# Stacking the high and low gate rows of the mLSTM into one matmul, and starting the output projection's buffers at multiples of 1 KB

## The reference

```python
def step(carry, xs):                      # one chunk of tokens, four heads
    b = jnp.cumsum(lfb, axis=-1)
    log_d = b[..., :, None] - b[..., None, :] + ib[..., None, :]
    log_d = jnp.where(causal, log_d, NEG)
    inter = b + m[..., None]
    m_t = jnp.maximum(jnp.max(log_d, axis=-1), inter)
    d_mat = jnp.exp(log_d - m_t[..., None])
    inter_w = jnp.exp(inter - m_t)
    s = jnp.einsum('bhtd,bhsd->bhts', qb, kb) * d_mat
    num = (jnp.einsum('bhts,bhsd->bhtd', s, vb)
           + inter_w[..., None] * jnp.einsum('bhvk,bhtk->bhtv', C, qb))
    ...
    C_new = decay[..., None, None] * C + jnp.einsum('bhs,bhsv,bhsk->bhvk', w, vb, kb)

mixed = jnp.concatenate([att.astype(x.dtype), ml, cv.astype(x.dtype)], axis=-1)
x = x + jnp.einsum('bse,ed->bsd', mixed, w_out[l])
```

## The kernel before

| tile | before | changed |
|---|---|---|
| `o_wh`, `o_wl`, `o_m`, `o_z`, `o_x` | 960 | 0 |
| `o_mh`, `o_ml`, `o_y` | 768 | 0 |
| moving operands of the spreads (`m_row_hi`, `m_row_lo`; then `m_row_parts`) | 0 | 256 |
| `m_mask_r` (moving, mask matmul) | 832 | 832 |
| `AHL`, `WH`, `WL` of the dense products | 0 | 0 |

## Time and profile before

### The profile page before, as it was taken

One profiled execution on the slowest core, in us unless ns is written; L12 is line 12 of the kernel. 1 busy time (PEld: TensorE's weight loads), 2 busy tenths in 40 slices (PEclk: granted clock), 3 DMA queues, 4 the chain that ended last, 5 costly groups with the idle time before them and its releaser, 6 DMA issues. The chain is left out here.

```text
span 3526.5 us, 43854 instructions
## 1 busy us (share of the span) xinstructions
PE 3339.7 (95%) x16481; PEld 2697.1 (76%) x16481; DVE 1839.3 (52%) x2219; ACT 1124.6 (32%) x1699; POOL 1436.1 (41%) x1006
## 2 busy tenths in 40 slices
PE   5877999999999999999999999999999999698899
PEld 5656878888888778888877888888778888376687
DVE  8785135544455776860125455455766860564421
ACT  4222133333333441112124333333541111566300
POOL 6810225656666322232225565666412231243421
PEclk9889999999999999999999999999999999898899
DMA  3344111111111222223211111111212231416543
GB/s 123 103 108 128 64 48 48 54 48 54 48 54 51 92 76 101 98 97 137 102 51 49 49 54 48 54 48 53 96 60 108 101 103 54 172 57 219 156 136 115
DMA packets 155316, 301.01 MB, mean 85 GB/s; under 512 B 16400, under 2 KB 91408, under 8 KB 153520
## 3 DMA queue, kind: packets, MB, share of 16 engines
q1 hardware_dynamic: 139056, 257.10, 22.9%
q10 hardware_dynamic: 16128, 42.08, 3.0%
HBM read 226.20 MB, written 72.94 MB: 85 GB/s over the span
## 5 line engine op out<-in xcount | busy, mean ns | idle before, releaser
L1721 PE MATMUL ps_job<-AHL,WH 128*128 128x512 f32 x4480 | 1382.1, 390 | 28.4 <-POOL WL L1290 26.8
L1290 POOL TENSOR_TENSOR WL<-WR,WH 128x1024 fp32r<-128x1024 f32 x216 | 523.0, 2422 | 1199.9 <-ACT WH L992 1198.4
L1721 PEld LDWEIGHTS ps_job<-AHL,WH 128*128 128x128 f32 x4480 | 840.8, 188 | 206.8 <-issue 19.0
L1721 PE MATMUL ps_job<-AHL,WL 128*128 128x512 f32 x2240 | 871.9, 389 | 0.0
L992 ACT CAST WH<-WR 128x1024 fp32r<-128x1024 f32 x216 | 226.9, 1051 | 1004.4 <-PE ps_job L1721 820.6
L1721 PEld LDWEIGHTS ps_job<-AHL,WL 128*128 128x128 f32 x2240 | 420.9, 188 | 87.4
L1481 DVE SCALAR_TENSOR_TENSOR ps_job<-ps_job,RB 128x1024 f32<-128x1024 f32 (+1 forms) x80 | 79.9, 1017 | 409.6 <-PE ps_job L1721 396.1
L1310 POOL TENSOR_TENSOR OPS_L<-VS,OPS_H 128x1024 fp32r<-128x1024 f32 (+2 forms) x96 | 193.9, 2036 | 55.8 <-ACT OPS_H L1118 51.3
L1400 DVE TENSOR_TENSOR VS<-ps_job,VS 128x1024 f32<-128x1024 f32 x16 | 19.6, 1225 | 362.3 <-PE ps_job L1721 362.3
L1818 PE MATMUL ps_job<-OPS_H,WH 128*128 128x512 f32 x512 | 199.5, 390 | 0.7 <-POOL WL L1290 0.7
L1818 PE MATMUL ps_job<-OPS_H,WL 128*128 128x512 f32 x512 | 199.3, 389 | 0.0
(11 more groups left out here) (428 smaller groups left out, 5732.8 us busy)
## 6 DMA issues: line engine op xcount, KB each, us to landing
WR<-in_wall SPq DMA_DIRECT2D x244, 512.0 KB, 3.5
fm_scratch<-VS ACTq DMA_DIRECT2D x32, 512.0 KB
tm_scratch<-VS ACTq DMA_DIRECT2D x28, 512.0 KB
s_U<-in_x_group SPq DMA_DIRECT2D x8, 1024.0 KB, 14.8
s_mt<-z_scratch SPq DMA_DIRECT2D x64, 128.0 KB, 4.5
prod_scratch<-s_Win SPq DMA_DIRECT2D x16, 512.0 KB, 2.6
X<-in_x_feat SPq DMA_DIRECT2D x2, 4096.0 KB, 14.8
m_oz<-tm_scratch SPq DMA_DIRECT2D x8, 1024.0 KB, 8.2
```

What stands on the lines that cost most here:

```text
L1290: pool.tensor_tensor(dst, raw, src.bitcast(F32), ALU.subtract).then_inc(raw_free, 1)
L1721: last = pe.matmul(out, l, r, start=(k == 0 and i == 0), stop=(k == k_tiles - 1 and i == 2))
```

## The change

Three things are done.

1. `load_pairs` brings each of the two row sets back from the DRAM scratch, twice: once into partitions 0 to 63 and once into partitions 64 to 127 of `m_row_pair0` and `m_row_pair1`. SP issues these four transfers in `attention`, behind the loads of the stage, and waits first until both stores of the rows have landed.
2. DVE makes the spread's operands 128 rows high: the high part in partitions 0 to 63 of `m_row_parts`, the low part in 64 to 127. For this it first adds two shifted pieces of the identity, and rounds both halves (the lower half into `m_row_hi`) before it subtracts. `spread` is then one matmul of 128 rows where it was two of 64.
3. `finish` places its buffers at multiples of 1 KB, and an unused buffer `o_w_pad` at the high end of SBUF does the same for those that come from there.

```diff
@@ attention
     env["weights"] = ExitStack()
+    env["weights"].enter_context(nc.sbuf_tensor("o_w_pad", [P, nc.sbuf_top % 1024 // 4], F32, side="right"))
     env["wh"] = wh = nc.alloc_sbuf_tensor_at("o_wh", [P, KD, D], F32R, offset=nc.sbuf_top)
...
             sp.dma_start(par[:], d["cv_par"]).then_inc(ld_p, 16)
+            rows.load_pairs(sp)
...
-            sp.wait_ge(rows.st, 32)
+            sp.wait_ge(rows.ld_pair, 64)
@@ GateRows
+        self.pair = [sb(f"m_row_pair{i}", [P, MC]) for i in range(2)]
...
+    def load_pairs(self, sp):
+        by_chunk = lambda v: v.rearrange("h (c n) -> (h c) n", n=MC)
+        sp.wait_ge(self.st, 32)
+        for i in range(2):
+            for part in range(2):
+                sp.dma_start(self.pair[i][part * self.n:(part + 1) * self.n], by_chunk(self.d["rows"][i])).then_inc(self.ld_pair, 16)
@@ mlstm_chunks
-            by_row = ident[0:R, 0:R].rearrange("p (h c) -> p h c", h=H)
...
+            dve.tensor_tensor(by_row[:], ident[:, high], ident[:, low], ALU.add).then_inc(of_set, 1)
...
-            for i, r in enumerate((rows.T, rows.B)):
+            for i, r in enumerate(rows.pair):
...
-                dve.tensor_copy(row_hi[i][:], by_head[i][:]).then_inc(row_set, 1)
-                dve.wait_ge(row_set, 3 * i + 2)
-                dve.tensor_tensor(row_lo[i][:], by_head[i][:], row_hi[i][:].bitcast(F32), ALU.subtract).then_inc(row_set, 1)
+                dve.tensor_copy(row_parts[i][high], by_head[i][high]).then_inc(row_set, 1)
+                dve.tensor_copy(row_hi[low], by_head[i][low]).then_inc(row_set, 1)
+                dve.wait_ge(row_set, 4 * i + 3)
+                dve.tensor_tensor(row_parts[i][low], by_head[i][low], row_hi[low].bitcast(F32), ALU.subtract).then_inc(row_set, 1)
...
             def spread(c, i, stop):
-                at = of_chunk[:, c:c + 1].to_broadcast([R, P])
-                pe.matmul(flat(e_ps[:]), at, flat(row_hi[i][:]), start=True, stop=False)
-                return pe.matmul(flat(e_ps[:]), at, flat(row_lo[i][:]), start=False, stop=stop)
+                return pe.matmul(flat(e_ps[:]), of_chunk[:, c:c + 1].to_broadcast([P, P]), flat(row_parts[i][:]), start=True, stop=stop)
@@ finish
-    sb, ps, sem = tools(nc, ctx)
+    sb, ps, sem = tools(nc, ctx, 1024)
```

More of the change, by code:

```diff
@@ L2417, in __init__ @@
         self.tok, self.dec = sb("m_tok", [P, N_MC, 3 * M_HEADS]), sb("m_dec", [P, M_HEADS, N_MC])
+        self.ld_pair = sem("m_ld_pair")
         self.ld, self.a_done, self.v_done, self.st, self.turned, self.tok_done = (
@@ L2537, in mlstm_chunks @@
     ident_r = sb("m_ident_r", [P, P], F32R)
-    of_head, in_chunk, of_chunk = sb("m_of_head", [R, H]), sb("m_in_chunk", [R, N_MC]), sb("m_of_chunk", [R, N_MC], F32R)
-    by_head = [sb(f"m_by_head{i}", [R, H, MC]) for i in range(2)]
-    row_hi, row_lo = ([sb(f"m_row_{n}{i}", [R, H, MC], F32R) for i in range(2)] for n in ("hi", "lo"))
+    by_row = sb("m_by_row", [P, R])
+    of_head, in_chunk, of_chunk = sb("m_of_head", [P, H]), sb("m_in_chunk", [P, N_MC]), sb("m_of_chunk", [P, N_MC], F32R)
+    by_head = [sb(f"m_by_head{i}", [P, H, MC]) for i in range(2)]
+    row_hi = sb("m_row_hi", [P, H, MC], F32R)
+    row_parts = [sb(f"m_row_parts{i}", [P, H, MC], F32R) for i in range(2)]
+    high, low = slice(0, R), slice(R, 2 * R)
+    assert 2 * R == P
     dn, rc = (sb(f"m_{n}", [P, 2, H]) for n in ("dn", "rc"))
@@ L2711, in _ @@
             dve.memset(state[:, 0], 0.0).then_inc(c_done, 1)
-            by_row = ident[0:R, 0:R].rearrange("p (h c) -> p h c", h=H)
-            dve.tensor_reduce(of_head[:], by_row, AX.X, ALU.add).then_inc(of_set, 1)
-            dve.tensor_reduce(in_chunk[:], by_row.rearrange("p h c -> p c h"), AX.X, ALU.add).then_inc(of_set, 1)
-            dve.wait_ge(of_set, 2)
+            dve.tensor_tensor(by_row[:], ident[:, high], ident[:, low], ALU.add).then_inc(of_set, 1)
+            dve.wait_ge(of_set, 1)
+            rows_of = by_row[:].rearrange("p (h c) -> p h c", h=H)
+            dve.tensor_reduce(of_head[:], rows_of, AX.X, ALU.add).then_inc(of_set, 1)
+            dve.tensor_reduce(in_chunk[:], rows_of.rearrange("p h c -> p c h"), AX.X, ALU.add).then_inc(of_set, 1)
+            dve.wait_ge(of_set, 3)
             dve.tensor_copy(of_chunk[:], in_chunk[:]).then_inc(of_set, 1)
-            for i, r in enumerate((rows.T, rows.B)):
-                dve.tensor_tensor(by_head[i][:], r[:, None, :].to_broadcast([R, H, MC]), of_head[:, :, None].to_broadcast([R, H, MC]),
+            for i, r in enumerate(rows.pair):
+                dve.tensor_tensor(by_head[i][:], r[:, None, :].to_broadcast([P, H, MC]), of_head[:, :, None].to_broadcast([P, H, MC]),
                                   ALU.mult).then_inc(row_set, 1)
-                dve.wait_ge(row_set, 3 * i + 1)
-                dve.tensor_copy(row_hi[i][:], by_head[i][:]).then_inc(row_set, 1)
-                dve.wait_ge(row_set, 3 * i + 2)
-                dve.tensor_tensor(row_lo[i][:], by_head[i][:], row_hi[i][:].bitcast(F32), ALU.subtract).then_inc(row_set, 1)
+                dve.wait_ge(row_set, 4 * i + 1)
+                dve.tensor_copy(row_parts[i][high], by_head[i][high]).then_inc(row_set, 1)
+                dve.tensor_copy(row_hi[low], by_head[i][low]).then_inc(row_set, 1)
+                dve.wait_ge(row_set, 4 * i + 3)
+                dve.tensor_tensor(row_parts[i][low], by_head[i][low], row_hi[low].bitcast(F32), ALU.subtract).then_inc(row_set, 1)
             def scores(c, s):
@@ L2772, in spread @@
             def spread(c, i, stop):
-                at = of_chunk[:, c:c + 1].to_broadcast([R, P])
-                pe.matmul(flat(e_ps[:]), at, flat(row_hi[i][:]), start=True, stop=False)
-                return pe.matmul(flat(e_ps[:]), at, flat(row_lo[i][:]), start=False, stop=stop)
+                return pe.matmul(flat(e_ps[:]), of_chunk[:, c:c + 1].to_broadcast([P, P]), flat(row_parts[i][:]), start=True, stop=stop)
             def exponents(c, s):
-                pe.wait_ge(row_set, 3)
-                pe.wait_ge(of_set, 3)
+                pe.wait_ge(row_set, 4)
+                pe.wait_ge(of_set, 4)
                 need(pe, dm_done, c)
@@ L2785, in row_weights @@
             def row_weights(c, s):
-                pe.wait_ge(row_set, 6)
+                pe.wait_ge(row_set, 8)
                 pe.wait_ge(dm_done, min(c + 2, N_MC))
```

## The result

| | before | changed |
|---|---|---|
| median of 5 runs on one chip (lowest, highest), us | 3531.17 (3529.8, 3534.2) | 3512.79 (3511.59, 3519.09) |
| the profiled execution, us | 3528.27 | 3519.09 |
| its span, us | 3526.5 | 3517.4 |

A forecast was written before the change was run, and what follows sets the result against it. PE was taken to bound both edited stretches, with ACT next in the mLSTM. Projection 5.0 plus mLSTM 6.2 (4.2 + 2.1 - 0.1) made 11.2 us off 3531.0: 3519.8 us, range 3514.5 to 3526.

The forecast's parts named there:

- Projection: Projection's matmuls: aligned buffers bring 233.3 ns a matmul down to the dense products' 226.7, gaining 5.0 us.
- The price of a spread: mLSTM `row_weights` and exponents' spreads: one 128-row matmul for two of 64 saves 0.32 us each, 0.64 a step.
- the ring: mLSTM step's waits from `row_weights` spread over ACT's `m_kw` and `m_dm` to the next spread: 6.31 us, becoming 5.99.
- What is late next: mLSTM steady part: ACT sets the pace, PE waits about 0.26 us a step; 0.38 us a step, 4.2 over eleven.
- ACT's idle time ahead of `m_kw`: Sign in the mLSTM step: ACT's idle time there falls from 0.94 us to about 0.6.
- Head and end: mLSTM steps outside the steady eleven: 0.8 us at chunk 1, then 0.65, 0.35 and 0.32, together 2.1 us.
- Transfers: Four added loads issued by SP in attention: 19 us of cover ahead of the first store, cost 0.
- Only the stacking: Rival: only the 128-row spreads gain, the projection's 233 ns having another cause; 3524.8 us, chance 0.17.
- PE sets the pace: Rival in the mLSTM: PE, not ACT, limits the step; 15.3 us off in all, 3515.7, chance 0.10.
- the transfers: Rival in the mLSTM: DMA transfers set the pace and the steady 4.2 us go; 3524.0 us, chance 0.13.
- clock rival: Rival: PE's pauses make the granted clock fall in the mLSTM; 8 us lost per 17 us stretch, 3536 from two, chance 0.04.
- the 0.1 I had taken off for the operand's start: mLSTM spread's operand now starts 256 bytes past a multiple of 1 KB: 0.1 us lost on the ring.

The follow-up runs named there:

- before again: The kernel before, profiled a second time with no edit: 3531.1 us in one run.
- two_of_128: Changed kernel with two matmuls a spread again, both 128 rows high, zeros filling the unused half: 3521.1 us, ratio 0.9972.
- one_of_64: Kernel before with only the 64-row `row_hi` matmul in each spread, low part left out: 3524.62 us in one run beside 3526.26.

## Why the prediction was right in its mechanisms and short in one size

- *Projection: right.* 5.0 forecast, 48 x 226.7 = 10.88 us a tile; measured 10.90, and 4.2 to 5.5 us over the stage, by the pair of profiles. The cause is the address of the moving operand, as assumed. That three touched pieces of 1 KB are what counts, and not being off a multiple in any way, was not tried.
- *The price of a spread: the step that failed.* I asked "is one matmul of 128 rows as quick as one of 64", answered by the mask's distance of 0.34, and took 0.32 a spread, on PE and on the ring alike. The new matmul itself came as forecast, with the next start 0.31 to 0.32 us later. But the mask's 0.34 was held up by the 64-row matmul in front, and in the changed kernel the mask takes 3246.81 - 3246.58 = 0.23. I had put the change of the row count at nothing, in front of a spread (0.53 against 0.35) and behind it (0.34 against 0.23). So a spread was worth 0.44 us on the ring. From the transposes to the first numerators PE lost 0.62: 3246.64 - 3245.12 = 1.52, now 3246.81 - 3245.91 = 0.90. PE's own sum fell not by 0.64 to 5.73 but by 1.23 to 5.14. The wait of 0.49 that the trace shows would leave 5.39, but it is counted from the modelled end of the last matmul.
- *What is late next: right in kind.* ACT's ring does set the step, with PE waiting ahead of the `row_weights` spread on `m_dm`: 0.49 us where I said 0.26. The ring is 1.84 + 3.89 + 0.15 = 5.88, not 5.99: 3.89 was exact, and where I had 2.28 - 0.32 = 1.96 it is 1.84. The steady part gained 5.4 us, not 4.2. ACT's idle time ahead of `m_kw`, 0.74 where I said 0.6, was no sign of this ring: one matmul less moves `m_wq` and `m_kw` alike, and the 0.20 that went is the row count's.
- *Head and end: 2.1 forecast, too low, for the most part from the same cause.* Compared at like half clock (before again and changed, 11.0 us each) the head gained 3.0 and the end 0.9. The spread's parts show in the head too: 30.0 before, 29.2 in `two_of_128`, 28.1 in `one_of_64` (10.1 of half clock), 27.0 changed. By this and by the ends (25.7, 25.5, 25.4 and 24.8) the row count is worth 0.9 us with two matmuls a spread and 1.7 with one. The first profile of before, with 17.0 us of half clock in its head, adds some 2 us that belong to no edit.
- *Transfers: right.* The four issues took 2.48 us on SP, in front of a store that went out 45.7 us into attention, 45.3 before; attention is 186.7 to 187.1 in the changed kernel and 186.6 and 187.1 before. In the mLSTM the DMA share rose from 0.80 to 0.88 and the waits for `m_oz` from 3.9 to 5.1 us, none on PE.
- *The rivals.* Only the stacking, PE sets the pace, and the transfers are each refuted by a row above. The time of "PE sets the pace", 3515.7, lies nearest to the 18 runs' 3516.2, by luck: PE did not set it. My clock rival did not occur: the steady part kept 1.00 with PE pausing in each step.
- *The sum.* At like half clock: 3.0 + 5.4 + 0.9 + 5.2 = 14.5 us, against 11.2. The two spans of this pair differ by 12.0, and the changed one began its attention 2.5 us later. The missing 3.3 are the price of a spread (1.2 in the steady part, and most of 1.8 in head and end), 0.2 of the projection, and the 0.1 I had taken off for the operand's start, for which no run shows a cost.
- *The range.* Its lower end, 3514.5, stood on a PE-bound step of 5.73, which the same wrong price set. And it left no room for the scatter of this kernel. The 14 profiles show 4.7 to 23.8 us at half clock between 400 us and attention. Attention begins at 3004.6 us in the one with 4.7, and at 3012.2 and 3012.6 in two with 23.8, whatever the edit. The changed kernel's 18 runs span 11 us, and its first median lies 3.4 under that of all. The three runs of the kernel before that I had seen span 3 us and hid this.

Open: why a pause of PE brings those stretches in one execution and not in the next of the same program, what part of the head's gain is the head's own timing, and why the half clock in the mLSTM's head lasts 17.0 us in one and 11.0 in another.

## What to carry to other kernels

When the price of an instruction is read off its neighbour, look at what stands in front of that neighbour: its weight load shows whether it could start early, and here a change of the row count on PE was paid by the next instruction. Write down the ring over each engine, not only PE's sum; here it named the new bound beforehand, and showed which engine's order to change next. Try a start at a multiple of 1 KB for rows that PE streams, and ask how far single runs scatter before setting the low end of a range.

## What the runs showed of the hardware that I had not expected

- A 128-row weight load is not pulled ahead of a 64-row matmul: 0.34 against 0.23 us for the matmul that follows, 1.64 against 1.44 us from the `row_weights` spread to the transposed keys. A 64-row load behind a 128-row matmul came late too: 0.53 against 0.35 us from the transposes to the spread. Doubling the rows of every spread, with as many matmuls, made the step 0.27 us shorter.
- With moving rows of 2 KB that start 960 bytes past a multiple of 1 KB a matmul took 233.3 ns, at a multiple 227.1. Moving the stationary operand's start from 768 bytes past one to a multiple changed nothing (11.20 us a tile both times).
- In the dense products, which the edit leaves alone, the granted clock fell to half for 3.4 or 6.8 us near 1210, 1852 and 2541 us in some executions of both kernels, each time within or right behind a pause of PE of 2.3 to 2.9 us, and not in others with the same pause.
